# First layer: the b matrices behind chunk 5 and the parameter rows behind chunk 6; operand transposes one slot up; the last feed-forward chunk's activations in two pieces

## The reference

```python
for l in range(DEPTH):                          # DEPTH = 2
    h = rms_norm(x, norm_mix[l])
    u_ssm, q_nsa, kv_nsa, g_nsa, qkv_sb, g_merge = split_columns(h @ w_in[l])
    o_ssm = s5_mixer(u_ssm, ...)                # diagonal complex state space, 32 groups of 16
    o_nsa = nsa_mixer(rope(q), rope(k), v, ...) # compressed, selected and window attention
    o_sb = stick_breaking_attention(...)        # weights from running sums of log sigmoids
    y = [o_ssm, o_nsa, o_sb] each @ w_branch[l]
    x = x + sum(sigmoid(g_merge) * y) @ w_out[l]
    x = x + conv_ffn(rms_norm(x, norm_ffn[l]), ...)   # D_FF 2816
return rms_norm(x, norm_final)

def conv_ffn(h, w_up, conv_w, conv_b, w_down):
    u = h @ w_up
    c = causal_depthwise_conv(u, conv_w, width=3) + conv_b
    gate, val = split(c)
    return (silu(gate) * val) @ w_down
```

```python
bb_re = f_re * b_re - f_im * b_im
bb_im = f_re * b_im + f_im * b_re
x = einsum(u, bb)            # then the scan over time with a = exp(lambda * step)
y = einsum(h_re, c_re) - einsum(h_im, c_im) + d_skip * u
```

## Time and profile before

| what | value |
|---|---|
| median of 3 runs | 948.28 us (947.02 to 948.35) |
| the profiled execution's own time | 950.34 us |
| its span in the trace | 948.6 us |
| PE busy | 98% of the span |
| DVE / ACT / POOL busy | 75% / 62% / 30% |
| TensorE's granted clock, mean over the span | 0.996 |
| weight queue q1, share of 16 DMA engines | 53.6% |
| moved | 159.09 MB, mean 168 GB/s |

### The profile page before, as it was taken

The page is one execution under the profiler, slowest core; times in us unless marked ns, Lnnn a source line. Parts: engine busy times, 40 slices in busy tenths (PEclk is TensorE's granted clock), DMA queues, the critical chain, the costliest instruction groups (busy, mean ns, idle before and its releaser), DMA issues.

```text
span 948.6 us, 16008 instructions
## 1 busy us (share of the span) xinstructions
PE 925.0 (98%) x5839; PEld 776.7 (82%) x5839; DVE 708.3 (75%) x1131; ACT 592.2 (62%) x956; POOL 289.2 (30%) x226
## 2 busy tenths in 40 slices
PE   8899999999999999999999999999999999999997
PEld 6889777777778888888879987777787788888886
DVE  6799967665667887898864977766657687777777
ACT  7445776768455765666665467677664566566655
POOL 0433324351420568467101413443316001010010
PEclk9999999999999999999999999999999999999999
DMA  9993433453554755556449844433645456556551
GB/s 221 247 269 98 147 123 132 132 150 129 167 176 138 219 192 193 177 185 213 139 123 264 233 154 134 133 117 106 180 131 178 133 178 207 193 177 205 191 179 45
DMA packets 139559, 159.09 MB, mean 168 GB/s; under 512 B 17153, under 2 KB 106089, under 8 KB 139498
## 3 DMA queue, kind: packets, MB, share of 16 engines
q1 hardware_dynamic: 137960, 156.44, 53.6%
q10 hardware_dynamic: 1538, 1.84, 0.7%
HBM read 154.33 MB, written 1.05 MB: 164 GB/s over the span
## 4 chain that ended last, share of the span: by engine, by line
PE 78%; DVE 9%; ACT 4%; SPq 3%; DMA 2%; issue 2%; ACTq 1%; POOL 0%; DVEq 0%; PEldq 0%; POOLq 0%
PE pj L801 57%; PE bX L801 7%; PE bA L801 6%; PE bB L801 4%; DVE wl L1733 3%; DMA ring<-in_w_in 2%; PE pj L1069 1%; ACT wh L1390 1%; SPq L618 1%; PE pj L1165 1%; SPq L671 1%; DVE gate L1758 1%; DVE s5a L1960 1%; DVE h L1765 1%; SPq L615 1%
## 5 line engine op out<-in xcount | busy, mean ns | idle before, releaser
L1733 DVE TENSOR_TENSOR wl<-ring,wh 128x1024 fp32r<-128x1024 f32 (+1 forms) x276 | 361.4, 1311 | 96.0 <-ACT wh L1390 94.8
L1390 ACT ACTIVATE wh<-ring 128x1024 fp32r<-128x1024 f32 (+1 forms) x276 | 288.2, 1045 | 154.4 <-PE pj L801 112.0
L801 PE MATMUL pj<-h,wh 128*128 128x256 f32 (+1 forms) x1376 | 296.6, 339 | 6.0 <-DVE wl L1733 5.0
L801 PE MATMUL pj<-wh,h 128*128 128x512 f32 (+1 forms) x832 | 259.6, 394 | 2.4 <-DVE h L1765 0.8
L801 PEld LDWEIGHTS pj<-h,wh 128*128 128x128 f32 x1376 | 230.6, 191 | 32.8 <-issue 7.0
L801 PE MATMUL pj<-h,wl 128*128 128x256 f32 x1024 | 189.0, 283 | 0.0
L801 PEld LDWEIGHTS pj<-wh,h 128*128 128x128 f32 x832 | 148.4, 188 | 41.5 <-issue 7.3
L801 PEld LDWEIGHTS pj<-h,wl 128*128 128x128 f32 x1024 | 157.6, 191 | 6.5
L801 PE MATMUL pj<-wl,h 128*128 128x512 f32 (+1 forms) x416 | 159.7, 384 | 0.0
L2422 POOL TENSOR_TENSOR work<-work 128x512 f32<-128x512 f32 x20 | 41.1, 2056 | 260.8 <-DVE work L2198 199.0
L801 PEld LDWEIGHTS pj<-wl,h 128*128 128x128 f32 x416 | 78.1, 188 | 16.3
(11 more groups left out here) (305 smaller groups left out, 1228.8 us busy)
## 6 DMA issues: line engine op xcount, KB each, us to landing
ring<-in_ffn_w_up SPq DMA_DIRECT2D x44, 1024.0 KB, 5.1
ring<-in_w_in SPq DMA_DIRECT2D x40, 1024.0 KB, 5.1
ring<-in_ffn_w_down SPq DMA_DIRECT2D x22, 1024.0 KB, 5.0
ring<-in_w_in SPq DMA_DIRECT2D x16, 512.0 KB, 5.5
ring<-in_w_branch SPq DMA_DIRECT2D x8, 1024.0 KB, 5.3
ring<-in_w_out SPq DMA_DIRECT2D x8, 1024.0 KB, 5.1
ring<-in_w_branch SPq DMA_DIRECT2D x8, 512.0 KB, 6.5
ring<-in_w_in SPq DMA_DIRECT2D x8, 256.0 KB, 3.4
```

The lines of the kernel that those rows point to most:

```text
L801: return nc.tensor.matmul(o, a, b, start=start, stop=stop, skip_group_check=True)
L1390: A(dst, src, ACT.Copy).then_inc(w_hi.sem, 1)
L1733: TT(dst, src, hi.bitcast(F32), ALU.subtract).then_inc(w_lo.sem, 1)
```

## The change

It has seven edits.

1. The two b matrices are no longer loaded with the other parameter matrices ahead of chunk 4, but in a function of their own, `load_b`, behind chunk 5, with a semaphore of their own, `b_in`.
2. The eleven rows transfers are issued behind chunk 6 instead of behind chunk 5.
3. In the first layer DVE's `s5_b` goes. POOL makes the products, sums and both spreads in this layer as well, with the functions that the second layer had already, and does so behind all four cosine products, instead of the spread and the products ahead of them and the second spread between the second and the third.
4. `S5_C` is 1 instead of 2 and `S5_B` is (2, 3) instead of (3, 4): PE's transposes, ACT's copies and DVE's diagonal that hang on these slots stand one slot earlier in the first layer. In the second layer's lists nothing of this moves.
5. At the second layer's start `split_lo(l, 1)` stands behind the last `x_down` and its turned rows instead of between the two.
6. The softplus of slot 36 stands between the two late gate copies of slot 35.
7. In the last feed-forward group ACT and DVE write the activations' two parts in two operations each, one for each 256 columns, and PE waits for the second half only when it comes to it.

```diff
@@ -141,7 +141,8 @@
 S5_Y = {s + 5 + (p == 5): p // 2 for s, p in S5_X.items() if p % 2}
-S5_C, S5_B = 2, (3, 4)
+S5_C, S5_B = 1, (2, 3)
+B_LATE, ROWS_LATE = 5, 6
@@ -398,7 +399,8 @@
         rows_in = sem("rows_in", 16 * 11)
-        mats_in = sem("mats_in", 16 * 6)
+        b_in = sem("b_in", 16 * 2)
+        mats_in = sem("mats_in", 16 * 4)
         params_free = sem("params_free", 1, 1)
@@ -429,7 +431,6 @@
         bx_ready = sem("bx_ready", 2)
-        b_made = sem("b_made")
         cx_ready = sem("cx_ready", 2)
@@ -490,8 +491,8 @@
         a_ready = sem("a_ready", STEPS)
-        a_hi = sem("a_hi", STEPS)
-        a_split = sem("a_split", STEPS, 2)
+        a_hi = sem("a_hi", STEPS + 1)
+        a_split = sem("a_split", STEPS + 1, 2)
         down_done = sem("down_done", 4)
@@ -704,9 +705,12 @@
+            def load_b(l):
+                for r, w in enumerate((ssm_b_re, ssm_b_im)):
+                    sp.dma_start(bnat[:, r], row(w, l).rearrange("l (t w) p i -> (w p) (l t) i", w=2))\
+                        .then_inc(b_in.sem, b_in.up(16))
             def load_mats(l):
-                for r, w in enumerate((ssm_b_re, ssm_b_im)):
-                    mat_in(bnat[:, r], row(w, l).rearrange("l (t w) p i -> (w p) (l t) i", w=2))
                 for r, w in enumerate((ssm_c_re, ssm_c_im)):
@@ -735,7 +739,9 @@
                     load(l, i)
-                    if l == 0 and i == 5:
+                    if l == 0 and i == B_LATE:
+                        load_b(0)
+                    if l == 0 and i == ROWS_LATE:
                         sp.wait_ge(setup.sem, 5)
@@ -772,6 +778,7 @@
                     load_rows(l + 1)
+                    load_b(l + 1)
                     load_mats(l + 1)
@@ -1318,6 +1325,7 @@
                         if t == 0 and k:
+                            pe.wait_ge(a_split.sem, a_split.at(l, STEPS + 1))
                             pe.wait_ge(w_lo.sem, w_lo.at(l, s + 2))
@@ -1392,7 +1400,7 @@
-                a.wait_ge(mats_in.sem, mats_in.at(0, 16 * 6))
+                a.wait_ge(mats_in.sem, mats_in.at(0, 16 * 4))
                 a.wait_ge(consts_in.sem, 16)
@@ -1685,8 +1693,9 @@
                         a.wait_ge(w_used.sem, w_used.at(l, s + 6) + turn * TURN)
-                    A(ah[:, :], aT[:, cc % 2, :], ACT.Copy).then_inc(a_hi.sem, 1)
-                    a_hi.made += times
+                    for c in ((slice(0, T), slice(T, 2 * T)) if cc == STEPS - 1 else (slice(0, 2 * T),)):
+                        A(ah[:, c], aT[:, cc % 2, c], ACT.Copy).then_inc(a_hi.sem, 1)
+                        a_hi.made += times
@@ -1879,15 +1888,6 @@
-            def s5_b():
-
-                v.wait_ge(mats_in.sem, mats_in.at(0, 16 * 6))
-                f, g = (both_planes(tiles_of(e, 0), GCH) for e in (fr, fi))
-                TT(bb[:, :], bnat[:, :], f, ALU.mult)
-                stepped(TT(bbt[:, :], bnat[:, :], g, ALU.mult))
-                TT(bb[:, 0], bb[:, 0], bbt[:, 1], ALU.subtract)
-                TT(bb[:, 1], bb[:, 1], bbt[:, 0], ALU.add).then_inc(b_made.sem, 1)
-
             for l in range(DEPTH):
@@ -1907,9 +1907,9 @@
                     turned_lo(l, 1, 0, 0, 0)
-                    split_lo(l, 1)
                     x_down(l - 1, 1, 1)
                     turned_lo(l, 2, 0, 1, JC)
+                    split_lo(l, 1)
                 norm_bias(n, 1)
@@ -1939,8 +1939,6 @@
                 split_lo(l, 8)
-                if l == 0:
-                    s5_b()
                 split_lo(l, 9)
@@ -2083,6 +2081,15 @@
+                def sb_softplus(k):
+                    v.wait_ge(z_ln.sem, z_ln.at(l, k + 1))
+                    if k:
+                        v.wait_ge(r_done.sem, r_done.at(l, k))
+                    for e in range(2):
+                        ins = STT(sbp[:, e, 0:384], (bA, bB)[e][:, 0:384], 0.0, sbw[k % 2][:, e, 0:384], ALU.max, ALU.add)
+                    ins.then_inc(z_sp.sem, z_sp.up())
                 if l:
@@ -2106,14 +2113,10 @@
                                 .then_inc(unit_out[n % 2].sem, unit_out[n % 2].up())
-                    if q in SB_P:
-                        k = SB_P[q]
-                        v.wait_ge(z_ln.sem, z_ln.at(l, k + 1))
-                        if k:
-                            v.wait_ge(r_done.sem, r_done.at(l, k))
-                        for e in range(2):
-                            ins = STT(sbp[:, e, 0:384], (bA, bB)[e][:, 0:384], 0.0, sbw[k % 2][:, e, 0:384], ALU.max, ALU.add)
-                        ins.then_inc(z_sp.sem, z_sp.up())
+                            if t == 0:
+                                sb_softplus(SB_P[q + 1])
+                    if q in SB_P and q != GATE_LATE + 1:
+                        sb_softplus(SB_P[q])
                     if q in S5_T:
@@ -2230,9 +2233,10 @@
                         split_lo(l, ffn_piece(1) + 3)
-                    v.wait_ge(a_hi.sem, a_hi.at(l, cc + 1) + turn * 2)
-                    TT(al[:, :], aT[:, cc % 2, :], ah[:, :].bitcast(F32), ALU.subtract).then_inc(a_split.sem, 1)
-                    a_split.made += times
+                    for n, c in enumerate((slice(0, T), slice(T, 2 * T)) if cc == STEPS - 1 else (slice(0, 2 * T),)):
+                        v.wait_ge(a_hi.sem, a_hi.at(l, cc + 1 + n) + turn * 2)
+                        TT(al[:, c], aT[:, cc % 2, c], ah[:, c].bitcast(F32), ALU.subtract).then_inc(a_split.sem, 1)
+                        a_split.made += times
                     if cc == STEPS - 1:
@@ -2269,7 +2273,7 @@
-                g.wait_ge(mats_in.sem, mats_in.at(l, 16 * 6))
+                g.wait_ge(mats_in.sem, mats_in.at(l, 16 * 4))
                 for c, mask in enumerate((K_PAR, K_NPAR)):
@@ -2289,6 +2293,7 @@
                 g.wait_ge(turns_ready.sem, 1)
+                g.wait_ge(b_in.sem, b_in.at(l, 16 * 2))
                 TT(bb[:, 0], bnat[:, 0], f, ALU.mult)
@@ -2333,20 +2338,18 @@
                 cos_b = kon[:, K_COS:K_COS + T].rearrange("p (o t) -> p o t", o=1)
-                if l == 0:
-                    g.wait_ge(b_made.sem, 1)
-                    g.wait_ge(consts_in.sem, 16)
-                    spread(bb, l, 0).then_inc(bx_ready.sem, bx_ready.up())
-                    products_ab(l)
-                    sums_ab()
                 for n, dst in enumerate((kr[:, 0:2, :], kr[:, 2:3, :], qr[:, 0:2, :], qr[:, 2:4, :])):
...
                         .then_inc(rot_cos.sem, rot_cos.up())
-                    if l == 0 and n == 1:
-                        spread_ab(l)
+                if l == 0:
+                    spread_b(l)
+                    products_ab(l)
+                    sums_ab()
+                    spread_ab(l)
```

## The result

| kernel | median | ratio to before, 95% interval |
|---|---|---|
| before | 948.32 us (6 runs, 947.02 to 948.84) | |
| changed | 955.51 us (6 runs, 953.36 to 956.58) | 1.0074 (1.0062 to 1.0085) |

The change costs 7.2 us by the medians. The forecast was 950.9 us, with a range of 946.0 to 954.8; the time lies 0.7 us above the range. The sign was right, the size was not. The profiled execution of the changed kernel took 955.58 us, that of before 950.34, so the two traces show only 5.2 of the 7.2 us: the profiled execution of before lay 2.0 us above its median, that of the changed kernel at its own.

What follows compares the result with a forecast made beforehand. PE was taken as the bound, busy 925.0 of 948.6 us. First layer's start +4.4, softplus -0.8, activations -0.5, second layer's start -0.5 made +2.6: 952.9 profiled, 950.9 us against the median, range 946.0 to 954.8.

Steps and rivals of the forecast that it cites:

- The vector engine beside POOL: First layer's start: DVE slowed by POOL's products loses 4.4 us (bounds 0 and 8.2), setting +4.4 us for the stage.
- rival B: First layer's start: DVE loses 41% of POOL's 20 us, 8.2; +6.4 in all, 954.7 us; chance 0.15.
- the term of the transfers: First layer's start: rows land 1.7 us later at the parameter transposes; the 1.93 us gap and clock fall go, 3.3 together.
- The start of its stretch does not move: First layer's start: DVE's stretch begins when it did, since its pieces wait for PE's use of three buffers.
- The slot and POOL's end: First b transposes: PE arrives at 74.5 us, POOL is done at 80.5, so PE stands still 6 us.
- rival A: First layer's start: POOL's chain takes 17 us, DVE loses a sixth of 13.4, effects cancel; 948.7 us; chance 0.22.
- The reference: Whole kernel: the profiled execution lies 2.1 us above the timed median 948.28, so 952.9 becomes 950.9 us.
- Softplus, activations, layer turn: Branch phase, last feed-forward chunks and second layer's start: gains of 0.8, 0.5 and 0.5 us.
- D: First layer's start: the clock falls again behind the first longer gap, delaying rotation and POOL by 1.4; 952.3 us; chance 0.15.
- three signs: Forecast wrong if POOL ends before 75 us, rows land before 42, or DVE's low parts keep 1.2 us beside POOL.

Runs made afterwards that it cites:

- pool_idle_work: Kernel before plus 20 unneeded POOL products of 128x256 behind the first layer's fourth cosine product; 958.60 us, ratio 1.0114.
- old_transfers: Changed kernel with edits 1 and 2 undone (b matrices ahead of chunk 4, rows ahead of chunk 6); 952.60 us, ratio 1.0048.
- small_rows_late: small_only with the eleven rows transfers behind chunk 6 and nothing else moved; 947.43 us, ratio 1.0000.
- small_only: Kernel before with edits 5, 6 and 7 alone, nothing of 1 to 4; 945.38 us, ratio 0.9971.
- slots_back: Changed kernel with S5_C and S5_B put back to 2 and (3, 4); 955.38 us, ratio 1.0085.
- pool_idle_wide: Kernel before plus 10 unneeded POOL products of 128x512 behind the first layer's fourth cosine product; 956.15 us, ratio 1.0091.

## Why the prediction was wrong

**The step that failed** is "The vector engine beside POOL": "I take a third of 13.4 us, 4.4 (bounds 0 and 8.2)". That DVE is the second clock of this stretch and sets the sum later than PE's own count was right, and it is where the time went; but DVE lost 8.1 us beside POOL's run (42.48 against 34.41), nearly twice the 4.4 and at the upper bound. Two things were wrong in the pricing. The rate came from long operations alone (a low part, 2.08 against 1.22 us), while more than half of the loss (4.3 us) sits in eight sums of 0.24 us, which grew by 0.53 us each. And the spreads were taken as free, since one row beside them kept its length; beside the second spread of the changed kernel (75.41 to 78.17) two table operations of 0.29 and 0.28 us took 0.58 and 0.70. Held against POOL's own time, 12.4 us, the forecast's 4.4 is a share of 0.35; measured were 8.1 or 0.65, and 0.83 in pool_idle_work. With 8.1 the forecast would have been 954.6 us, close to rival B's 954.7 and still inside the range. The second step is the term of the transfers, which had been put at nothing ("The start of its stretch does not move") and cost 2.5 us. With it, less the 0.9 us that the three small edits gained beyond their forecast, the sum comes to 956.2, 0.7 us too many and as near as the medians can tell.

The operations on b were miscounted as 16. They are 18 (6, 4, 2, 2 and 4, as the order lists them); the 20 units of 0.62 us and their 12.4 us are right, so no sum changes.

The Trainium skill ("SBUF — State Buffer", "SBUF: two separate sides") has the shared pair of ports as an exclusive lock that blocks the loser for a whole instruction. The forecast named that rule with +12.4 us as its price and then did not give it a chance of its own. The trace bears out the larger part of it: DVE lost 8.1 of the 12.4 us, and 10.3 of 12.4 in pool_idle_work, more than half and less than all.

**Transfers.** That the rows land late was forecast well (43.8 us; the trace has 43.99), and the 1.93 us gap went. The price was wrong in sign: 1.7 us late against 3.3 us regained was to be a gain, and it was a loss of 2.5 us (old_transfers) or 2.7 (small_rows_late, rows alone). The gap was 5.38 us and not about 4. Of the 3.3 us regained, 1.38 were the clock's fall in the one profiled execution, which small_only doesn't show behind the same gap, and the rest was not PE's to keep, since it waits for DVE later. The late rows, on the other hand, hold back DVE as well. "The start of its stretch does not move" held in the changed kernel's trace (61.61 against 61.47 us for the same low part), but that trace of before is a late one. The first eight sums start at 57.33 in the changed kernel and at 57.19 in it, and at 54.85 to 56.61 in the seven other traces with the old order of the transfers and POOL's work on b not moved ahead of the rotation. So what the transfers cost, some 2 us at this place, doesn't show between the two traces of the result.

**The slot and POOL's end.** POOL was to be done at 80.5 us, with PE standing still for 6 us ahead of the b transposes. It was done at 78.17, since its run took 17.1 us and not 20.0 (rival A's figure), and PE came to them only at 80.24, having waited 2.53 us for the sums. The chain was slower on the waiting side and faster on the awaited one, so this gap did not come about, and slots_back shows that undoing it is worth nothing.

**The reference.** The forecast took 2.1 us off for the profiled execution's place above its median. It added the change's sum to that, though 1.38 us of what the change was to remove (the clock's fall) may well be a part of those 2.1 us. A cost that only the profiled execution shows can't be gained back against the median.

**Softplus, activations, layer turn.** -1.8 us were forecast, -2.7 measured. From 202.08 to 267.16 is 65.08 us before, and 64.41 from 210.28 to 274.69 now: the softplus gives 0.7 us in a layer and not only the 0.40 us of its gap. The activations give 0.3 in each layer, as forecast (0.3 and 0.26). The layer turn shows 0.9 us between the two traces against the 0.5 forecast; but the stretch that follows it differs by 1.3 us between executions of kernels with the same code there, so this share is not settled.

**The rivals.** B (DVE loses 8.2 us) and D (the clock falls behind the new gaps) both came about, in one kernel. They had been priced singly, and the range ended at the dearer one alone. D is seen in the windows of the three gaps above. The two falls behind 73 and 87 us added nothing to the sum: PE's piece at 105.14 stands 8.21 us behind that at 96.93 before, just as DVE's low part ahead of it does (103.86 against 95.65). The fall behind 43.99 can have made DVE's start later; how much of the transfers' 2.5 us is its share stays open. The six executions of the changed kernel took 953.4 and 953.8 us where the mean granted clock was 0.996, and 955.4 to 956.6 us at 0.992 to 0.994. So 2 to 3 us go along with the clock, but longer gaps would lengthen the time and lower the clock together, and no experiment holds the two apart.

None of the three signs that the forecast named for being wrong came about: POOL ended at 78.17 and not before 75, the rows landed at 43.99 and not before 42, and the low parts took 1.64 and 1.72 us and not 1.2. They looked at the long operations, and more than half of the loss sat in eight short ones.

## What to carry to other kernels

Work for a second engine isn't free because that engine is idle: ask which engine sets the pace at the time when it will run. The same 18 POOL operations cost 1.4 us, hardly told from nothing, while transfers set the pace, and 5.6 us more when moved 23 to 33 us later, beside a vector engine without a pause. Price such an overlap by the operations that will stand there, the short ones above all, and when two rivals can happen together, price them together before drawing the range.

## What was not expected of the hardware

- Short vector operations lose most beside POOL: 0.24 us became 0.78 beside products of 128x256, while a 1.22 us operation became 1.6 to 1.8.
- POOL copies with one input disturb the vector engine as well: 3.5 us for 8.0 us of them, against 10.3 us for 12.4 us of products.
- A gap of 1.93 us of PE was followed by a lower granted clock in one execution and one of 1.96 us by the full clock in another; at the parameter transposes the row took 0.90 us instead of 0.55 behind gaps of 5.38 and 5.95 us, and in pool_idle_wide behind one of 2.47 us too, while behind the 2.42 us of the earlier trace rows it took 0.55 and behind 2.78 us in old_transfers 0.56.
